# Two transformer blocks on one core: inversions begun over unit matrices laid by another engine, a state decayed ahead, gates scaled in mid-turn, and reordered edges of two stages

## What is computed

```python
def step(S, inp):
    r_t, w_t, k_t, v_t, kk_t, a_t = inp
    sa = jnp.einsum("bhvk,bhk->bhv", S, kk_t)
    S = (S * w_t[:, :, None, :]
         - sa[..., None] * (kk_t * a_t)[:, :, None, :]
         + v_t[..., None] * k_t[:, :, None, :])
    return S, jnp.einsum("bhvk,bhk->bhv", S, r_t)
```

## Time and profile before

| | |
|---|---|
| median of 3 runs | 2370.06 us (2370.05 to 2371.14) |
| profiled execution | 2369.44 us, span 2367.4 us |
| PE busy | 2321.1 us, 98% |
| DVE, ACT, POOL busy | 1573.1, 523.5, 416.5 us |
| chain that ended last | PE 92%, DVE 4%, ACT 3%, issue 1% |
| TensorE clock granted | full, but for 6.8 us after 2106 us |

### The profile page before, as it was taken

The page is one execution under the profiler, slowest core; times in us unless marked ns, Lnnn a source line. Parts: engine busy times, 40 slices in busy tenths (PEclk is TensorE's granted clock), DMA queues, the critical chain, the costliest instruction groups (busy, mean ns, idle before and its releaser), DMA issues.

```text
span 2367.4 us, 54497 instructions
## 1 busy us (share of the span) xinstructions
PE 2321.1 (98%) x23796; PEld 2026.1 (86%) x23796; DVE 1573.1 (66%) x3091; ACT 523.5 (22%) x1217; POOL 416.5 (18%) x483
## 2 busy tenths in 40 slices
PE   8999999999999999999999999999999999999999
PEld 8999888899999998888999888478888889556558
DVE  7886675388768867753888787456666666147652
ACT  2101030111011010301110100234444443032341
POOL 1111000011011110001223320233444441100000
PEclk9999999999999999999999999999999999999999
DMA  7555554445555554545455322023233334312112
GB/s 280 192 178 196 178 184 155 160 169 191 193 178 187 186 194 170 191 158 178 162 191 183 112 86 90 0 44 62 53 54 57 57 56 97 99 53 89 55 53 71
DMA packets 169453, 310.22 MB, mean 131 GB/s; under 512 B 108992, under 2 KB 134768, under 8 KB 135296
## 3 DMA queue, kind: packets, MB, share of 16 engines
q1 hardware_dynamic: 165024, 278.02, 36.3%
q0 software_dynamic: 4192, 28.72, 3.4%
HBM read 293.06 MB, written 13.63 MB: 130 GB/s over the span
## 4 chain that ended last, share of the span: by engine, by line
PE 92%; DVE 4%; ACT 3%; issue 1%; DMA 0%; SPq 0%; POOL 0%; DVEq 0%; ACTq 0%; POOLq 0%
PE psum L700 28%; PE psum L1075 21%; PE psum L1136 12%; PE psum L1244 6%; PE psum L718 5%; PE psum L1347 3%; PE psum L1336 2%; PE psum L1349 2%; PE psum L1438 1%; PE psum L1046 1%; PE psum L1434 1%; PE psum L1596 1%; PE psum L1364 1%; DVE arena L2770 1%; PE psum L1638 1%; ACT arena L1921 1%
## 5 line engine op out<-in xcount | busy, mean ns | idle before, releaser
L700 PE MATMUL psum<-arena,ring 128*128 128x256 f32 (+1 forms) x2864 | 675.2, 395 | 8.5 <-ACT arena L1744 8.3
L700 PEld LDWEIGHTS psum<-arena,ring 128*128 128x128 f32 x2864 | 541.8, 190 | 130.0 <-issue 56.7
L1075 PE MATMUL psum<-arena 128*128 128x128 f32 x2560 | 325.1, 275 | 0.0
L1075 PEld LDWEIGHTS psum<-arena 128*128 128x128 f32 x2560 | 305.1, 192 | 0.0
L1075 PE MATMUL psum<-arena,ring 128*128 128x128 f32 x1920 | 253.6, 275 | 0.0
L1075 PEld LDWEIGHTS psum<-arena,ring 128*128 128x128 f32 x1920 | 233.9, 192 | 0.2
L2336 DVE TENSOR_TENSOR arena<-ring 128x1024 f32<-128x1024 f32 x136 | 171.0, 1257 | 38.7 <-PE psum L1136 34.9
L1136 PE MATMUL psum<-arena 128*128 128x128 f32 x1408 | 184.7, 275 | 0.0
L1136 PEld LDWEIGHTS psum<-arena 128*128 128x128 f32 x1408 | 170.7, 192 | 0.0
L2358 DVE SCALAR_TENSOR_TENSOR arena<-arena 128x256 f32<-128x256 f32 x336 | 164.0, 529 | 5.1
L1347 PE MATMUL psum<-arena 64*64 64x64 f32 x2560 | 158.5, 223 | 7.2 <-DVE arena L2770 5.6
(11 more groups left out here) (335 smaller groups left out, 3333.3 us busy)
## 6 DMA issues: line engine op xcount, KB each, us to landing
ring<-in_weights SPq DMA_DIRECT2D x238, 1024.0 KB, 4.9
arena<-in_ada POOLq DMA_DIRECT2D x24, 1024.0 KB, 5.2
squares<-arena SPq DMA_DIRECT2D x128, 96.0 KB, 2.1
arena<-squares SPq DMA_DIRECT2D x128, 64.0 KB, 2.6
arena<-squares SPq DMA_DIRECT2D x128, 32.0 KB, 2.6
arena<-in_const POOLq DMA_DIRECT2D x1, 1312.0 KB, 6.3
arena<-in_x SPq DMA_DIRECT2D x1, 1024.0 KB, 4.8
ring<-in_weights SPq DMA_DIRECT2D x2, 512.0 KB, 6.9
```

What stands on the lines that cost most here:

```text
L700: mm = self.nc.tensor.matmul(out, self.ring[:, slot % RING, i * P:(i + 1) * P], rhs, start=(kc == 0), stop=(kc == len(moving) - 1))
L1075: mm = nc.tensor.matmul(bank[:, n * P:(n + 1) * P], left[:, kind, pair, :], right[:, pair, :], start=(n == 0 and pair == 0), stop=(n == la ...
```

## The change

- **Unit matrices.** ACT's new `lay_ones(q+1)` at the head of each turn copies unit matrices over both matrices of an inversion (one instruction of 128x512, one of 128x256). `begin_inverse` waits for them and then writes the masked products over them with two `copy_predicated`, in place of four `tensor_tensor`. The masks are 1 where they were -1. The sign is made up for: the scale of a is -0.5, ka is negated, and take_u has no scale.
- **State.** `update_state` is two `scalar_tensor_tensor` of 128x64 (new part times decay, plus the state decayed before), then a wait for them, then `decay_state`: two `tensor_scalar` of 128x64 that multiply the state by the decay of the next step.
- **Gates.** The scaling of w and a is cut from take_gates and becomes `finish_gates`, in the middle of turns with g = 0 (w) and g = 1 (a). The exponentials move from the head and the middle of g = 1 to its middle and its end. The first "w" of pair 1 moves from the middle of turn 0 to before the turns.
- **Start of the recurrence.** next_inverse(0, 1) stands two pieces earlier, lower_product(0, 2) inside the last gate product rather than behind it; turn_squares(0) stands ahead of begin_inverse(0).
- **End of the recurrence.** Two pieces of rw_out stand ahead of the state_product of step 62.
- **Last stage.** The gate product g 0 moves ahead, among the last rotations; all later ones move up by one. o_scale 0 to 3 stand between g 6 and g 7, and 4 to 7 behind g 7, ahead of the last product. silu is taken over g 0 to 5 at once, and of g 6 and 7 straight from PSUM.
- **Small.** One more memset and one more tensor_scalar before the recurrence; a memset on DVE stands a little earlier in the last unit of rkv.

```diff
+    if place == "ahead":
+        names += [("w", 1, 0, "act"), ("w", 1, 1, "act")]
     if place == "middle":
-        if q == 0:
-            names += [("w", 1, 0, "act"), ("w", 1, 1, "act")]
...
             for kc in range(DC):
-                if kc == DC // 2:
+                if kc == 2:
                     next_inverse(0, 1)
+                if kc == 6:
+                    lower_product(0, 2)
                 mm = st.piece(last_gate, h2[:, kc, :], kc == 0, kc == DC - 1)
             mm.then_inc(s.bank_full, 1)
-            lower_product(0, 2)
...
             st.all_banks_empty(SCAN)
+            side(0, "ahead")
...
+            some(2, pieces)
             for k in (2 * TURNS - 2, 2 * TURNS - 1):
                 state_product(k)
...
+            def lay_ones(q):
+                b, one = q % 2, c_view("one")
+                if q >= 2:
+                    act.wait_ge(s.xy_full[b], level_count(q - 2, LEVELS - 1))
+                nc.scalar.activation(xy[:, b, :, :, :].rearrange("p i u t -> p (i u) t"),
+                                     one.unsqueeze(1).to_broadcast([P, 8, CHUNK]), ACT.Copy)
+                nc.scalar.activation(lt_all[:, b, :, :], one.unsqueeze(1).to_broadcast([P, 4, CHUNK]),
+                                     ACT.Copy).then_inc(s.ones_laid[b], 1)
             def side_head(q):
-                if g == 1 and n < PAIRS:
-                    exponentials(n, 0)
+                if 2 <= q + 1 < TURNS:
+                    lay_ones(q + 1)
...
             def side_middle(q):
-                if q == 0:
-                    take_gates("w", 1)
+                if g == 0 and pair + 1 < PAIRS:
+                    finish_gates("w", pair + 1)
                 if g == 1 and pair + 1 < PAIRS:
-                    exponentials(pair + 1, 1)
+                    finish_gates("a", pair + 1)
+                    exponentials(pair + 1, 0)
...
             def side_tail(q):
...
+                if g == 1 and pair + 1 < PAIRS:
+                    exponentials(pair + 1, 1)
...
             def begin_inverse(q):
                 b = q % 2
+                dve.wait_ge(s.ones_laid[b], q // 2 + 1)
                 dve.wait_ge(s.first_gram_full, q + 1)
-                tt(xy_, ps_first[b], minus_pairs, ALU.mult)
-                link(tt(lt_, ps_first[b][:, 1, :, :], mask("minus_earlier"), ALU.mult))
-                xy_ = xy_.rearrange("p i u t -> p (i u) t")
-                tt(xy_, xy_, mask("one", 8), ALU.add)
-                tt(lt_, lt_, mask("one"), ALU.add).then_inc(s.inverse_begun[b], 1)
+                nc.vector.copy_predicated(xy[:, b, :, :, :], pairs0, ps_first[b])
+                nc.vector.copy_predicated(lt_all[:, b, :, :], mask_bits("earlier"),
+                                          ps_first[b][:, 1, :, :]).then_inc(s.inverse_begun[b], 1)
...
-                link(tt(s_state, psum[:, 0, 384:512].rearrange("p (u t) -> p u t", u=2), s_state, ALU.add))
-                tt(s_state, s_state, p_end[:, pair % 2, :, step:step + 1].to_broadcast([P, 2, HEAD]),
-                   ALU.mult).then_inc(s.s_updated, 1)
+                for d in range(2):
+                    ins = stt(s_state[:, d, :], psum[:, 0, 384 + d * HEAD:384 + (d + 1) * HEAD],
+                              p_end[:, pair % 2, d, step:step + 1], s_decayed[:, d, :], ALU.mult, ALU.add)
+                ins.then_inc(s.s_updated, 1)
+                dve.wait_ge(s.s_updated, k + 2)
+                decay_state(k + 1)
+            def decay_state(k):
...
+                for d in range(2):
+                    ins = ts(s_decayed[:, d, :], s_state[:, d, :], p_end[:, pair % 2, d, step:step + 1], None, ALU.mult)
+                link(ins)
...
-            gate_of(2)
+            gate_of(3)
             turned_probs(HALVES - 1)
-            gate_of(3)
+            gate_of(4)
             attend(DA_HEADS - 1)
-            gate_of(4)
+            gate_of(5)
             sums_of_o(DA_HEADS - 1)
-            gate_of(5)
             gate_of(6)
-            scale_of_o(0)
-            scale_of_o(1)
+            for h in range(4):
+                scale_of_o(h)
             gate_of(7)
-            scale_of_o(2)
-            scale_of_o(3)
+            for h in range(4, DA_HEADS):
+                scale_of_o(h)
```

More of the change, by code:

```diff
@@ L442, in scan_order @@
     o = Order(SECOND_A, main=(6, 7))
+    for *name, by in scan_tiles(0, "ahead"):
+        o.add(tuple(name), by)
     for q in range((PAIRS + 1) * GROUPS):
@@ L492, in second_b_order @@
             o.add(("o_sums", (i - 3) // 2), "act")
-    for name in (("g", 2), ("probs_turned", HALVES - 1), ("g", 3), ("o", DA_HEADS - 1), ("g", 4), ("o_sums", DA_HEADS - 1),
-                 ("g", 5), ("g", 6), ("o_scale", 0), ("o_scale", 1), ("g", 7), *(("o_scale", h) for h in range(2, DA_HEADS))):
+    for name in (("g", 3), ("probs_turned", HALVES - 1), ("g", 4), ("o", DA_HEADS - 1), ("g", 5), ("o_sums", DA_HEADS - 1),
+                 ("g", 6), *(("o_scale", h) for h in range(4)), ("g", 7), *(("o_scale", h) for h in range(4, DA_HEADS))):
         o.add(name, "dve" if name[0] in ("o", "o_scale") else "act")
@@ L617, in __init__ @@
         self.s_updated = new("s_updated")
+        self.ones_laid = [new(f"ones_laid_{b}") for b in range(2)]
 class Arena:
@@ L858, in build @@
     squares_turned = Arena(arena, second.at).take(6, 4, SQUARE)
+    s_decayed = Arena(arena, second.at + 6 * 4 * SQUARE).take(2, HEAD)
     lora_lo = second.take(2, T2)
@@ L1676, in _ @@
             mean_square_of(last)
+            gate_of(0)
             turned(last - 1)
@@ L1988, in _ @@
             take_gates("w", 0)
+            finish_gates("w", 0)
             take_gates("a", 0)
+            finish_gates("a", 0)
             act.wait_ge(s.slot_used, LAST_PART_LEFT)
@@ L1994, in _ @@
             take_gate(3 * DC + 1)
+            lay_ones(0)
+            lay_ones(1)
             for m in range(3 * DC + 2, 4 * DC - 1):
@@ L2609, in _ @@
             link(ts(one_minus_ka, ka, -1.0, 1.0, ALU.mult, ALU.add))
+            link(ts(ka, ka, -1.0, None, ALU.mult))
             link(ts(half_b, p2[:, P2["w0"]:P2["w0"] + 4 * DC], 0.5, None, ALU.mult))
@@ L2639, in _ @@
                 first_, second_ = shift_pad[:, 0, :, 1:T + 1], shift_pad[:, 1, :, 1:T + 1]
+                if u == RKV_UNITS - 1:
+                    dve.wait_ge(s.slot_used, RING + FIRST_SLOTS + u + 1)
+                    nc.vector.memset(lora_of, 0.0).then_inc(s.lora_zeroed, 1)
                 dve.wait_ge(s.rkv_p1, u + 1)
@@ L2647, in _ @@
                 else:
-                    dve.wait_ge(s.slot_used, RING + FIRST_SLOTS + u + 1)
-                    nc.vector.memset(lora_of, 0.0).then_inc(s.lora_zeroed, 1)
                     link(nc.vector.memset(restart, 1.0))
@@ L2676, in _ @@
             nc.vector.memset(s_state, 0.0).then_inc(s.s_updated, 1)
+            dve.wait_ge(s.lora_in, 4)
+            link(nc.vector.memset(s_decayed, 0.0))
             def sum_decays(n):
@@ L2806, in _ @@
             begin_inverse(1)
-            dve.wait_ge(s.lora_in, 4)
-            turn_squares(0)
             for q in range(TURNS):
```

71 lines of the change are left out of this document (44 added, 27 removed).

## The result

The changed kernel takes 2346.88 us (median of 4 runs, 2345.68 to 2347.53) against 2370.06 (2366.79 to 2371.14): ratio 0.9902, 95% interval 0.9889 to 0.9914. The forecast was 2352 in a range of 2341 to 2363, faster: right, with 23.2 us won by the medians and 21.9 by the two profiled executions (spans 2367.4 and 2345.5) where 18.0 were forecast. The sum was near; its shares were not, and the runs show that.

What follows compares the result with a forecast made beforehand. PE, busy nearly all of the 2367.4 us span, was taken as the bound, so only its waits could be won. Gains and losses in the recurrence, tail and last stage summed to 18.0 us: 2352 us, range 2341 to 2363.

Steps and rivals of the forecast that it cites:

- Gates and exponentials: At take_u, freed from ACT's queue: 0.79 us won in each g = 1 turn and 0.2 in g = 0.
- Unit matrices: In begin_inverse, two copies of 0.68 and 0.42 us end both waits of g = 2: 1.63 us won per turn.
- State, g = 1: state_product(k+1) no longer late through update_state waiting for POOL: 0.68 us won per turn, none if the second decay meets POOL.
- State, g = 2: The first step's decay falls into POOL's directions and delays the mask behind it: 1.3 us lost, seven times.
- State, plain turns: The longer update uses all the 0.30 slack before the next mask: 0.05 us on some 20 turns, 1.0 lost.
- Turns 0 and 1: Waits at the start of the recurrence go: 2.9 us won in turn 0 and 2.9 in turn 1.
- Tail and last stage: Two pieces fill idle time behind the turns, 0.75 us won; the idle before the last product goes, 1.3 won.
- POOL's cover: POOL's later directions end at 11 us, the next pair's first_gram is due at 13.3: 2.2 us cover, no cost.
- A: Rival: the state's decays on DVE do not meet POOL, or hide; 28 us won, 2342 us, chance 0.15.
- B: Rival: DVE's longer state update decides every turn; 5 to 12 us left, 2361 us, chance 0.22.
- C: Rival: copy_predicated in begin_inverse, covered to about 1.5 us, is slower; 2364 us at the scan's rate; chance of slower 0.05.
- signs named beforehand: Trace signs of being right, among them, in g = 2, next_inverse's second run idle behind a tensor_scalar of 1 us or more.

Runs made afterwards that it cites:

- experiment 3: Changed kernel with the gates' scaling and the exponentials at their old places, ones still laid at the head of each turn; 2363.91 us.
- kernel 5: Changed kernel with the state's update and begin_inverse both as before and no ones laid, so gates and exponentials moved alone, edges changed; 2345.07 us.
- kernel 7: Changed kernel with gates, exponentials and begin_inverse as before, so only the state decayed ahead, edges changed; 2366.71 us.
- experiment 1: Changed kernel with the state updated as before (add the product, then scale by the decay; nothing decayed ahead); 2342.72 us.
- experiment 4: Changed kernel with the order at the start of the recurrence as before; 2346.63 us.
- experiments 4 and 9: experiment 4 has its own line; 9 is the changed kernel with the tail of the recurrence and the last stage as before, 2346.96 us.

## Why the prediction was right in sum and wrong in its shares

That the sum came within 4 us is in part luck: two large terms were off by 7 to 13 us each, in opposite directions.

By the steps of the prediction, forecast against what the runs give for it:

- **Gates and exponentials** (4.7 in g = 1, 1.0 in g = 0, 2.1 of turn 1: about 8). Measured 18.3 to 20.4. This step was right in its mechanism, take_u freed, and its 0.79 is contained in g = 1's 1.41 (forecast 1.47); experiment 3 gives 1.62 with the ones in the queue. Its 0.2 in g = 0 was the net of 0.90 won (15.17 to 14.27 in kernel 5) and 0.53 lost to the ones; 0.37 came. What it left out is what the same move does through POOL: the directions start at 1801.51, behind the update, and the second run at 1810.42, where it meets fewer of DVE's additions. That is the other half of g = 1, which the prediction counted under the state though it had the later start of the directions in hand, and nearly half of the 1.63 of g = 2 (14.93 to 14.20 in kernel 5), which it counted under the matrices.
- **Unit matrices** (6 x 1.63 = 9.8). Measured 2.0 to 2.5. The prices of the two copies were right, 0.75 and 0.43 for 0.68 and 0.42. The step that failed priced the removed waits by the old positions of POOL, though another part of the same change moves POOL. With the old positions it would have held in g = 2: 14.83 to 13.45 from kernel 7 to kernel 3, 1.38 a turn. There, though, the ones take back 0.83 in g = 0. I had put the ones at a cost of 0.9 on ACT, near in size (0.83 from the first one's start to the next instruction's). In g = 0 they hold take_u, 0.53 a turn.
- **State, g = 1** (0.68 each and 0.77 in turn 1). The time came, but from the gates: with the old update the turn is even shorter (14.44 against 14.57, experiment 1). "This operand pair is gone" explains nothing; in kernel 7, where POOL stands as before, the decays wait as the scaling did.
- **State, g = 2** (-1.3, seven times). The mis-sized term of the sum: 0.42 in six turns and 1.04 in turn 2, which is 5.5 us less than forecast, more than the whole difference between 18.0 and 21.9. "Each of two neighbours waits for one POOL instruction" did not hold here: taken singly, the decays of turn 18 took 0.57 and 0.24.
- **State, plain turns** (-1.0). 0.11 to 0.13 in each of some twenty, -2.4: the step from update to mask grew by 0.43 where 0.3 was put, against the slack of 0.30. The sizes by the slope of 1.04 ns a column were right (0.28, two in 0.46 to 0.48). The figure by the formula in the Trainium skill (VectorE: DVE Perf Modes, "The TRN2 errata"), 0.19 us for 64 columns, was low; the trace has 0.27 to 0.28.
- **Turns 0 and 1** (2.9 each). 2.24 and 2.63. In turn 0 the 0.76 before next_inverse(1, 2) stands where the prediction had counted 0.9 won for kv's wait. DVE's order at this place is unchanged, and mask 2 comes 2.59 behind mask 5 in both kernels, as the two scans (2.33) stand between them; before, kv's wait of 0.80 had covered that. So one wait went and uncovered another. The start's order alone is worth 2.0 (experiment 4), and all of turn 1's gain comes with the gates (13.70 in kernel 5).
- **Tail and last stage** (2.05). 2.4 in the profiled executions, which had the same granted clock; 2.3 by experiments 4 and 9.
- Not seen at all: kv's wait of 0.95 in turn 28. Among the kernels here with the same code at that place it is anywhere from 0 to 0.95; why is open.
- POOL's cover (2.2 us) was underestimated by a misread row: at 1836.1 next_inverse 2 begins, and first_gram only at 1836.99. Nothing hung on it.

Of the rivals, A (decays that hide) was nearer than the forecast in g = 2: of a pair, the second often does not wait. B came in small: the update cost PE 0.13 in a plain turn where B had 0.2, and in the middle of g = 1 the decays don't meet POOL in the changed kernel (they do in kernel 7). C's point was at 1.7 to 2.2 us, and the copies took 1.1. The Trainium skill (SBUF — State Buffer, "Who interferes with whom") spoke against the decays on DVE beside POOL, and the trace agrees in g = 2 (0.57 for a decay that takes 0.25 alone). The state's part is also the one that cost time, 1.8 to 3.9 us, but most of that is its length in plain turns, where POOL has no share; in g = 2 the old scaling waits for POOL too.

Of the signs named beforehand one came out otherwise: ahead of the late mask in g = 2 stands a tensor_scalar of 0.57, not of 1 us or more.

So the errors met in the middle: 10 to 13 us too few for the gates (10 to 11 without turn 28 and the lower clock of turn 1), 7 to 8 too many for the copies, a cost of 4.6 for the state where 1.8 to 3.9 are measured.

## What to carry to other kernels

Where a change moves one engine's work, price the other parts of it against the engines' new positions: the waits that a part removes may be gone already, and only kernels with one part undone tell whose gain it was. Ask of every helper instruction which engine has a gap there, and put it in that gap, as with the decays and the ones, which lost time on DVE and at the head of a turn and won it behind take_o. A wait between two products of one shape was not won here by filling it with a product of another shape.

## What the runs showed of the hardware

copy_predicated of 128x512 with data from PSUM and a mask from SBUF took 0.69 to 0.76 us and 128x256 0.42 to 0.46, and never waited for POOL, not even where POOL was in the middle of an instruction, and not when issued three times.

Of two short tensor_scalars from SBUF to SBUF beside POOL, the first waited until POOL's running instruction was over in 21 of the 27 pairs of the changed kernel that began with at least 0.27 us of one left; the other six all began inside L2276, a tensor_scalar of POOL's, and took 0.26. Whether the second waits goes with the gap between POOL's instructions: in the changed kernel it never did (16 pairs of 48 in which the first took over 0.4, the second never over 0.25), and POOL's next instruction began 0.08 to 0.11 behind the one before. In experiment 3, where POOL's L950 and L951 follow each other without that gap, both waited, in six turns. DVE's pair at the end of turn 17 there, where it has cover, and POOL:

```profile
1820.94 1.70 DVE L2851 TENSOR_SCALAR arena<-arena 128x64 f32<-128x64 f32 x2
```

```profile
1820.18 1.18 POOL L950 TENSOR_TENSOR ring<-arena 128x512 f32<-128x512 f32 x1
1821.31 1.28 POOL L951 TENSOR_TENSOR arena<-arena 128x512 f32<-128x512 f32 x1
```

And around the end of one wait of 3.6 us on PE the granted clock fell to the lower level for 6.8 us, for 3.4 us or not at all, in kernels with the same code at that place; 6.8 us of it cost 2.9, more than several of the parts here.
